# Last two output tiles of a two-block transformer kernel in token stretches of 256, 128 and 128

## What is computed

```python
def rms_norm(x, g):
    xf = x.astype(jnp.float32)
    y = xf * lax.rsqrt(jnp.mean(xf * xf, axis=-1, keepdims=True) + EPS)
    return (y * g.astype(jnp.float32)).astype(x.dtype)

def second_block(x, c, norm_g, w_ada, b_ada, w_in, ...):
    ...
        y = jnp.concatenate([y_a, y_b], axis=-1) @ w_out[l]
        x = x + gate[:, None, :] * y
    return rms_norm(x, final_g)
```

## Time and profile before

| | us |
|---|---|
| median of 3 runs | 2403.07 (2402.24 to 2403.16) |
| profiled execution, its own time | 2403.81 |
| its span | 2401.7 |
| TensorE busy | 2355.8 (98%) |
| VectorE busy | 1260.8 (52%) |
| ScalarE busy | 875.3 (36%) |
| GpSimd busy | 421.9 (18%) |
| matmul of 512 columns, mean duration | 0.389 |

### The profile page before, as it was taken

The page is one execution under the profiler, slowest core; times in us unless marked ns, Lnnn a source line. Parts: engine busy times, 40 slices in busy tenths (PEclk is TensorE's granted clock), DMA queues, the critical chain, the costliest instruction groups (busy, mean ns, idle before and its releaser), DMA issues.

```text
span 2401.7 us, 31321 instructions
## 1 busy us (share of the span) xinstructions
PE 2355.8 (98%) x11378; PEld 1957.5 (82%) x11378; DVE 1260.8 (52%) x1965; ACT 875.3 (36%) x1335; POOL 421.9 (18%) x409
## 2 busy tenths in 40 slices
PE   7999999999999999999999999999999999999998
PEld 6888888888887888888788887788878888887887
DVE  8655452477556556443467777553264444444334
ACT  5422222365225322222365223422234444444221
POOL 5111100043113111100042112212002222222000
PEclk9999999999999999999999999999999999999999
DMA  7554553212322555543212223423222222223232
GB/s 278 172 184 167 191 169 115 69 59 71 105 96 71 197 175 171 186 167 131 79 53 71 96 90 111 159 87 105 96 79 88 80 78 79 79 73 133 102 103 79
DMA packets 80906, 281.90 MB, mean 117 GB/s; under 512 B 8896, under 2 KB 13248, under 8 KB 79936
## 3 DMA queue, kind: packets, MB, share of 16 engines
q1 hardware_dynamic: 63968, 217.49, 26.5%
q0 software_dynamic: 16864, 63.45, 7.7%
HBM read 272.51 MB, written 8.39 MB: 117 GB/s over the span
## 4 chain that ended last, share of the span: by engine, by line
PE 83%; issue 8%; DVE 6%; ACT 2%; POOL 0%; DMA 0%; ACTq 0%; DVEq 0%
PE bank L341 26%; PE bank L342 26%; PE bank L343 26%; DVE w_lo L335 1%; PE bank L2172 1%; ACT w_hi L312 1%; DVE bank L1576 1%; PE bank L2081 1%; DVE x_res L1151 0%; PE bank L2252 0%; PE bank L2095 0%; DVE q_rope L1459 0%; PE bank L2253 0%; DVE x_lo L1245 0%; DVE mix_lo L1582 0%
## 5 line engine op out<-in xcount | busy, mean ns | idle before, releaser
L343 PE MATMUL bank<-x_hi,w_hi 128*128 128x512 f32 x2896 | 1125.9, 389 | 0.0
L342 PE MATMUL bank<-x_hi,w_lo 128*128 128x512 f32 x2896 | 1125.7, 389 | 0.0
L341 PE MATMUL bank<-x_lo,w_hi 128*128 128x512 f32 (+1 forms) x2384 | 941.6, 395 | 8.0 <-POOL x_lo L418 3.4
L335 DVE SCALAR_TENSOR_TENSOR w_lo<-w_raw,w_hi 128x1024 fp32r<-128x1024 f32 x383 | 474.2, 1242 | 728.3 <-ACT w_hi L312 727.1
L312 ACT ACTIVATE w_hi<-w_raw 128x1024 fp32r<-128x1024 f32 x390 | 407.6, 1048 | 929.2 <-PE bank L343 903.1
L343 PEld LDWEIGHTS bank<-x_hi,w_hi 128*128 128x128 f32 x2896 | 544.2, 188 | 114.0
L342 PEld LDWEIGHTS bank<-x_hi,w_lo 128*128 128x128 f32 x2896 | 545.0, 188 | 107.7 <-issue 2.2
L341 PEld LDWEIGHTS bank<-x_lo,w_hi 128*128 128x128 f32 x2384 | 448.5, 188 | 100.9 <-issue 6.6
L341 PE MATMUL bank<-mix_lo,w_hi 128*128 128x512 f32 (+1 forms) x656 | 254.9, 389 | 0.8 <-issue 0.5
L425 POOL TENSOR_SCALAR probs<-probs,stats 128x128 f32<-128x128 f32 (+3 forms) x128 | 143.8, 1130 | 636.4 <-DVE stats L1565 636.4
L431 POOL DMA_DIRECT2D ada_w<-wada x96 | 52.7, 549 | 537.1 <-DVE ada_w L1020 536.0
(11 more groups left out here) (341 smaller groups left out, 2165.6 us busy)
## 6 DMA issues: line engine op xcount, KB each, us to landing
w_raw<-stream SPq DMA_DIRECT2D x390, 512.0 KB, 3.5
ada_w<-wada POOLq DMA_DIRECT2D x96, 512.0 KB, 4.8
x_tokens<-xN SPq DMA_DIRECT2D x4, 1024.0 KB, 7.9
x_res<-xT SPq DMA_DIRECT2D x16, 256.0 KB, 10.7
x_res_spill<-x_res POOLq DMA_DIRECT2D x8, 512.0 KB, 6.5
x_res<-x_res_spill POOLq DMA_DIRECT2D x8, 512.0 KB, 7.1
outT<-x_res SPq DMA_DIRECT2D x16, 256.0 KB, 2.2
cond_b<-cond POOLq DMA_DIRECT2D x2, 1024.0 KB, 6.3
```

The source lines that it names most:

```text
L335: nc.vector.scalar_tensor_tensor(out=WL[:, slot, :cols[n]], in0=RAW[:, slot, :cols[n]], scalar=1.0, in1=WH[:, slot, :cols[n]].bitcast(F32) ...
L341: nc.tensor.matmul(out, wh, xl, start=first, stop=False)
L342: nc.tensor.matmul(out, wl, xh, start=False, stop=False)
L343: return nc.tensor.matmul(out, wh, xh, start=False, stop=last)
```

## The change

The token halves become three stretches, `LAST_BLOCKS`: tokens 0 to 255, 256 to 383, 384 to 511. Tiles 14 and 15 are made in six parts, two of 48 matmuls of 256 columns and four of 48 matmuls of 128 columns. Each stretch has its own sums, root, diagonal and spread.

The sum over features is taken in two steps on TensorE: `first_sums` adds the running sum without the last tile's square, inside the odd part after input 12; `rms_sums` adds the last tile's square straight from `SQ`. So VectorE adds one square per stretch (`last_sum`), not two.

GpSimd multiplies tiles 0 to 13, all 512 columns, by their norm weights as soon as ScalarE has squared them. `scale_out` then multiplies several of these tiles by the spread bank in one plain operation (two tiles of 256 columns in the first stretch, four tiles of 128 in the others); tiles 14 and 15 keep the old form. SyncE stores 16 times as before, 256 KB each, eight times two tiles of 256 columns and eight times four tiles of 128, in which a run of one tile and one partition in memory is 512 bytes and no longer 1024.

```diff
 HALF = NT // 2
-LAST_PARTS = ((KT - 2, 0, 2), (KT - 1, 0, 5), (KT - 2, 1, 0), (KT - 1, 1, 1))
+LAST_BLOCKS = ((0, 1), (2,), (3,))
+LAST_PARTS = [(KT - 2 + n, e, (2, 5, 0, 1)[(2 * e + n) % 4]) for e in range(3) for n in range(2)]
+LAST_SPREADS = (6, 7, 4)
+GROUPED = (2, 4, 4)
...
+        def stretch(e):
+            return slice(P * LAST_BLOCKS[e][0], P * (LAST_BLOCKS[e][-1] + 1))
+
+        def scale_groups(e):
+
+            size = GROUPED[e]
+            return [(k, min(k + size, KT - 2)) for k in range(0, KT - 2, size)] + [(KT - 2, KT - 1), (KT - 1, KT)]
+
+        def scaled(e, k):
+
+            before = sum(len(scale_groups(n)) for n in range(e))
+            return before + [end for _, end in scale_groups(e)].index(k) + 1
...
-            for h in range(2):
-                for m in range(0, KT, 2):
-                    sp.wait_ge(S["fin"], KT * h + m + 2)
-                    sp.dma_start(outT[m:m + 2, :, tokens(h)].rearrange("k p n -> p k n"), Y2[:, m:m + 2, tokens(h)])\
-                        .then_inc(S["stored"], 16)
-            sp.wait_ge(S["stored"], 16 * KT)
+            for e, size in enumerate(GROUPED):
+                for m in range(0, KT, size):
+                    sp.wait_ge(S["fin"], scaled(e, m + size))
+                    sp.dma_start(outT[m:m + size, :, stretch(e)].rearrange("k p n -> p k n"),
+                                 Y2[:, m:m + size, stretch(e)]).then_inc(S["stored"], 16)
+            sp.wait_ge(S["stored"], 16 * sum(KT // size for size in GROUPED))
...
+            for k in range(KT - 2):
+                pool.wait_ge(S["r_sq"], k + 1)
+                nc.gpsimd.tensor_scalar(Y2[:, k, :], Y2[:, k, :], column(EXT, E_FG + k), None, ALU.mult)\
+                    .then_inc(S["h_mul"], 1)
...
-            for n, (m, h, bank) in enumerate(LAST_PARTS):
+            for n, (m, e, bank) in enumerate(LAST_PARTS):
+                c = stretch(e)
                 act.wait_ge(S["out2_ev"], KT - 2 + n + 1)
-                act.wait_ge(S["r_sum"], KT - 2 + n)
-                nc.scalar.activation(SQ[:, tokens(h)], Y2[:, m, tokens(h)], ACT.Square).then_inc(S["r_sq"], 1)
+                act.wait_ge(S["r_sum"], KT - 2 + (e + 1 if n % 2 else 0))
+                nc.scalar.activation(SQ[:, c], Y2[:, m, c], ACT.Square).then_inc(S["r_sq"], 1)
                 if n % 2:
-                    rms_sd(h)
+                    rms_sd(e)
 
 
...
             def last_part(n):
-                m, h, bank = LAST_PARTS[n]
+                m, e, bank = LAST_PARTS[n]
+                c = stretch(e)
                 dve.wait_ge(S["part_mm"], n + 1)
-                STT(out=Y2[:, m, tokens(h)], in0=PS[bank][:, tokens(h)], scalar=column(MOD, 2 * KT + m),
-                    in1=Y2[:, m, tokens(h)], op0=ALU.mult, op1=ALU.add).then_inc(S["out2_ev"], 1)
-                dve.wait_ge(S["r_sq"], KT - 2 + n + 1)
-                dve.wait_ge(S["r_sum"], KT - 2 + n)
-                TT(out=A1[:, tokens(h)], in0=A1[:, tokens(h)], in1=SQ[:, tokens(h)], op=ALU.add).then_inc(S["r_sum"], 1)
-
-            def scale_out(h, ks):
-                for k in ks:
-                    STT(out=Y2[:, k, tokens(h)], in0=Y2[:, k, tokens(h)], scalar=EXT[:, E_FG + k:E_FG + k + 1],
-                        in1=PS[6 + h][:, tokens(h)], op0=ALU.mult, op1=ALU.mult).then_inc(S["fin"], 1)
+                STT(out=Y2[:, m, c], in0=PS[bank][:, c], scalar=column(MOD, 2 * KT + m),
+                    in1=Y2[:, m, c], op0=ALU.mult, op1=ALU.add).then_inc(S["out2_ev"], 1)
+
+            def last_sum(e):
+                c = stretch(e)
+                dve.wait_ge(S["r_sq"], KT - 2 + 2 * e + 1)
+                dve.wait_ge(S["r_sum"], KT - 2 + e)
+                TT(out=A1[:, c], in0=A1[:, c], in1=SQ[:, c], op=ALU.add).then_inc(S["r_sum"], 1)
+
+            def scale_out(e, groups):
+                c = stretch(e)
+                width = P * len(LAST_BLOCKS[e])
+                for g in groups:
+                    k, end = scale_groups(e)[g]
+                    if k < KT - 2:
+                        dve.wait_ge(S["h_mul"], KT + end)
+                        by = PS[LAST_SPREADS[e]][:, c].rearrange("p (k n) -> p k n", k=1)\
+                            .broadcast_to([P, end - k, width])
+                        TT(out=Y2[:, k:end, c], in0=Y2[:, k:end, c], in1=by, op=ALU.mult).then_inc(S["fin"], 1)
+                    else:
+                        STT(out=Y2[:, k, c], in0=Y2[:, k, c], scalar=EXT[:, E_FG + k:E_FG + k + 1],
+                            in1=PS[LAST_SPREADS[e]][:, c], op0=ALU.mult, op1=ALU.mult).then_inc(S["fin"], 1)
...
-            def rms_sums(h):
-                pe.wait_ge(S["r_sum"], KT + 2 * h)
-                for t in (2 * h, 2 * h + 1):
-                    last = mm(PS[3][:, t:t + 1], A1[:, t * P:(t + 1) * P], ONES[:, 0:1], start=True, stop=True)
+            def first_sums(e):
+                pe.wait_ge(S["r_sum"], KT - 1 + e)
+                for t in LAST_BLOCKS[e]:
+                    mm(PS[3][:, t:t + 1], A1[:, t * P:(t + 1) * P], ONES[:, 0:1], start=t == LAST_BLOCKS[e][0],
+                       stop=False)
+
+            def rms_sums(e):
+                pe.wait_ge(S["r_sq"], KT - 2 + 2 * e + 2)
+                for t in LAST_BLOCKS[e]:
+                    last = mm(PS[3][:, t:t + 1], SQ[:, t * P:(t + 1) * P], ONES[:, 0:1], start=False,
+                              stop=t == LAST_BLOCKS[e][-1])
                 last.then_inc(S["r_mm"], 1)
 
-            def rms_spread(h):
-                pe.wait_ge(S["r_dg"], QB + 2 * h + 2)
-                mm(PS[6 + h][:, tokens(h)], ONES[:, :], DG[1][:, 2 * h:2 * h + 2, :].rearrange("p t n -> p (t n)"),
+            def rms_spread(e):
+                blocks = LAST_BLOCKS[e]
+                pe.wait_ge(S["r_dg"], QB + blocks[-1] + 1)
+                mm(PS[LAST_SPREADS[e]][:, stretch(e)], ONES[:, :],
+                   DG[1][:, blocks[0]:blocks[-1] + 1, :].rearrange("p t n -> p (t n)"),
                    start=True, stop=True).then_inc(S["r_bc"], 1)
...
-                m, h, bank = LAST_PARTS[n]
+                m, e, bank = LAST_PARTS[n]
+                c = stretch(e)
                 if n >= 2:
-                    pe.wait_ge(S["out2_ev"], KT - 2)
+                    pe.wait_ge(S["out2_ev"], KT - 2 + max(n - 3, 0))
...
-                    last = products(PS[bank][:, tokens(h)], WH[:, slot, col0:col0 + P], WL[:, slot, col0:col0 + P],
-                                    xh[:, tokens(h)], xl[:, tokens(h)], k == 0, k == KT - 1)
+                    last = products(PS[bank][:, c], WH[:, slot, col0:col0 + P], WL[:, slot, col0:col0 + P],
+                                    xh[:, c], xl[:, c], k == 0, k == KT - 1)
...
-            for n in range(4):
-                out_part(n, {6: [do(rms_sums, 0)], 15: [do(rms_spread, 0)]} if n == 2 else {})
-            fill(8)
-            rms_sums(1)
+            for n in range(2 * len(LAST_BLOCKS)):
+                e = n // 2
+                if n % 2:
+                    out_part(n, {12: [do(first_sums, e)]})
+                elif n:
+                    out_part(n, {8: [do(rms_sums, e - 1)], 15: [do(rms_spread, e - 1)]})
+                else:
+                    out_part(n, {})
+            fill(5)
+            rms_sums(2)
             fill(3)
-            rms_spread(1)
+            rms_spread(2)
```

More of the change, by code:

```diff
@@ L843, in _, with rms_sd @@
                 layer(l)
[L846 to L849, removed]
+            def rms_sd(e):
+                c = slice(LAST_BLOCKS[e][0], LAST_BLOCKS[e][-1] + 1)
+                act.wait_ge(S["r_v"], e + 2)
+                nc.scalar.activation(ST[:, 24:28][:, c], ST[:, 20:24][:, c], ACT.Sqrt).then_inc(S["r_sd"], 1)
             def half_split(s, n, i=0):
@@ L1127, in rms_sum, with rms_end @@
                     TT(out=A1[:, :], in0=A1[:, :], in1=SQ[:, :], op=ALU.add).then_inc(S["r_sum"], 1)
-            def rms_end(h):
-                c = slice(2 * h, 2 * h + 2)
-                dve.wait_ge(S["r_mm"], 2 + h)
+            def rms_end(e):
+                blocks = LAST_BLOCKS[e]
+                c = slice(blocks[0], blocks[-1] + 1)
+                dve.wait_ge(S["r_mm"], 2 + e)
                 TS(ST[:, 20:24][:, c], PS[3][:, c], 1.0 / D, RMS_EPS, ALU.mult, ALU.add).then_inc(S["r_v"], 1)
-                dve.wait_ge(S["r_sd"], 2 + h)
+                dve.wait_ge(S["r_sd"], 2 + e)
@@ L1135, in rms_end @@
                 V.reciprocal(ST[:, 28:32][:, c], ST[:, 24:28][:, c]).then_inc(S["r_ri"], 1)
-                dve.wait_ge(S["r_ri"], 2 + h)
-                for t in (2 * h, 2 * h + 1):
+                dve.wait_ge(S["r_ri"], 2 + e)
+                for t in blocks:
                     TS(DG[1][:, t, :], IDN[:, :], ST[:, 28 + t:29 + t], None, ALU.mult).then_inc(S["r_dg"], 1)
             def last_part(n):
-                m, h, bank = LAST_PARTS[n]
+                m, e, bank = LAST_PARTS[n]
+                c = stretch(e)
@@ L1821, in _ @@
             last_part(0)
+            last_sum(0)
```

(41 more changed lines are left out.)

## The result

The changed kernel takes 2408.90 us (median of 16 runs, 2406.70 to 2409.95) against 2403.19 (16 runs, 2401.18 to 2404.64): 5.7 us more, a ratio of 1.0023 with a 95% interval of 1.0016 to 1.0030. Forecast were +6.7 us and 2409.8. The span of the profiled execution is 2407.3 us, 5.6 more than before.

A forecast was written before the change was run, and what follows sets the result against it. TensorE bounds the kernel up to its last product, then VectorE and the stores in a 14.9 us tail. TensorE +11.41 and tail -4.70 give +6.7 us, 2409.8 us; range 2407.0 to 2413.0.

The forecast's parts named there:

- The narrow parts: TensorE, tiles 14 and 15, last 256 tokens: 192 matmuls of 128 columns paced by weight loads, 0.1125 us each, plus 10.08 us.
- What stands between: TensorE, inside the parts: ten records of sums and two of a spread added, 12 x 0.111 = 1.33 us more.
- The tail: From the first fill behind TensorE's last product to the span's end: 14.93 to 10.23 us, a gain of 4.70.
- A store: Output stores at the end, runs of 512 bytes: 1.0 us per store instead of 0.78, so the last five queue.
- A group of 512 elements: VectorE's grouped scaling at the end: 0.69 us each, with bounds of 0.69 and 1.04.
- The rival in which the tail gains more: Tail without a store queue, all at lower bounds: gains 5.3 us; same mechanism but under 4.8 us slower, 5 in 100.
- GpSimd: Its 14 multiplications, 0.85 us each, one per tile, cost the path nothing; last done some 15 us before its first reader.
- the price on VectorE: VectorE's running sum beside GpSimd takes 1.19 instead of 0.69 us, covered by idle time; without it 7 us due.
- The clock: Rival: TensorE's clock falls to 1.2 GHz in the narrow parts, 2411.5 us if for 3.4 us, 2431 throughout; 5 in 100.
- VectorE's backlog: Kernel before: four leftover scalings of the first half delay the last part's addition from 2387.0 to 2388.9.

The follow-up runs named there:

- half weights: The changed kernel with the four narrow parts' weights cut to 64 of 128 columns: 2397.23 us in its one run, distance between starts 0.059 us.
- half columns: The changed kernel with the four narrow parts computing only 64 of their 128 columns, weight loads unchanged: 2426.86 us in its one run.

## Why the prediction was right

**The narrow parts** were forecast at 21.60 us for 192 matmuls. Measured are 23.16 from part 2 to the fills, less ten one-column records and the two of the narrow spread at 0.111 each and the wide spread of 0.41: 21.4, that is 0.1115 us each. That four distances in another stage of the kernel gave this is what the forecast rests on, and half weights and half columns show its reason to be true. The Trainium skill (TensorE: Matmul & The Clock Gate, Back-to-back issue gap) gives about 81 ns for such pairs, by which the change would have made no difference; this case's trace disagrees, with 0.1115 us for these weights.

**What stands between** was forecast at +1.33 us. Four of its records lie in parts 0 and 1 (11.95 us to the start of part 2, before 11.51). Both terms together measured +11.22 (35.11 - 23.89) against +11.41, and with the tail's -5.30 the sum is +5.92 where +6.7 was forecast; the two errors have the same sign, so none hid the other.

**The tail** was forecast at 10.23 us and took 9.63. Its path was right: the last five stores queue behind each other, and 0.87 us are left after them. Their data start 4.21 us after the first fill (2401.88 - 2397.67), not 4.38; of this the two records of sums, 0.28 us and not 0.40, are a part. A store took (2406.43 - 2401.88) / 5 = 0.91 us, not 1.0, which gives the other 0.45. A group of 512 elements follows the one before in 0.60 us, not 0.69 (the duration stands in the row, but VectorE starts the next before the last has ended, which the earlier trace rows show for the single scalings and I did not carry over); as the stores are the slower side, this changed nothing. The store did get slower than the 0.78 of before, by less than I forecast: a fixed part for each run, sized from loads of 4096 and stores of 1024 bytes, gave 0.032 us for a run of 512 bytes on one engine (its 0.0355 per KB should read 0.036, which leaves the 0.032), and 0.91 / 32 = 0.028 were measured. The rival in which the tail gains more named 5.3 us as its bound without a queue at the stores; 5.30 were gained, with the queue in place. The Trainium skill (DMA: Bandwidth & Descriptors, Specifications) has 512 bytes at line rate; the trace disagrees, with 284 to 290 GB/s against 333 at 1024 bytes.

**GpSimd** was mis-sized. I took 0.85 us from L444, whose instruction multiplies by a constant and adds a column; the change's takes 2.05. The rows of the same form (a column as the only factor, L425, 1.13 us on the mean of four widths and 1.66 at 512 columns) would have been nearer. And the price on VectorE was put on the wrong operation: the running sum kept its 0.693 us, the low part after it rose from 1.23 to 1.37. VectorE's idle time before L1843 stayed at 39.9 us, and what was lost came out of the idle time before the low part (39.0 us instead of 40.8). That it cost the path nothing shows in the change's trace while GpSimd works: TensorE is busy for all of the 140 us, as before.

```profile
2222.00:2362.00 140.00, 140.00 (x619) 116.00 (x618) 51.98 (x53) 34.37 (x39) 26.59 (x13) 1.00 0.27 90
```

**The clock** stayed at 1.00 up to 2402 us, so its chance of 5 in 100 went unused; the half-column kernel shows that the doubt was due. How close the change comes to that fall was not tried.

**VectorE's backlog** was read rightly as 1.8 us of the tail before; moving four scalings took 1.6 off it (14.93 to 13.35). What I did not do is ask what it would take to remove it alone: the order of four instructions.

## What to carry to other kernels

Before cutting matmuls narrower to start a tail earlier, find in the trace the distance between starts at the new width with the same weights: here it hardly fell any more from 256 to 128 columns (0.120 to 0.1115 us), and such a cut doubles a cost instead of sharing it. Set that against the tail, term by term, and look first for queued work that can be put behind the critical instruction at no cost. Where a tail ends in stores that fill the DMA engines, faster arithmetic in front of them brings little: here 1.5 us less on VectorE shortened the tail by 0.6.

## What the runs showed that I had not expected

- In matmuls of 64 columns, each with a load of 128x128 weights, TensorE was busy all the time, and yet its granted clock fell from 1.00 to 0.50, and the distance between starts went from 0.11 to 0.21 us (one run). With 128 columns it stayed at 1.00 over 23 us.
- On GpSimd the same multiplication of 128x512 by a column takes 2.05 us as one operation and 1.17 us as times 1.0, then times the column.
- VectorE's 128x1024 operation of two inputs took 1.37 instead of 1.23 us beside GpSimd, while a 128x512 sum of two inputs that overlapped with GpSimd for nearly its whole length kept its 0.69; it was GpSimd's operation that grew, by 0.27 us against one beside a copy.
- Full DMA engines stored 284 to 290 GB/s in runs of 512 bytes, 333 in runs of 1024 and up to 364 in runs of 1536.
